# Modulation products cut by column group and turned by VectorE, with two early blocks of layer 1 in the slots of the gate weights

## What is computed

```python
def modulation(cvec, w_ada, b_ada):
    m = jax.nn.silu(cvec) @ w_ada + b_ada
    return jnp.split(m, 6, axis=-1)
...
        sh1p, sc1p, g1p, sh2p, sc2p, g2p = modulation(c_ctx, w_ada[i], b_ada[i])
        sh1s, sc1s, g1s, sh2s, sc2s, g2s = [m[:, None, :] for m in modulation(c, w_ada[i], b_ada[i])]
        hp = rmsnorm(xp, norm_g[i, 0]) * (1.0 + sc1p) + sh1p
        hs = rmsnorm(xs, norm_g[i, 0]) * (1.0 + sc1s) + sh1s
```

## Time and profile before

| | us |
|---|---|
| median of 3 runs | 1181.83 |
| lowest and highest of them | 1177.47, 1183.61 |
| span of the profiled execution | 1179.7 |
| start and first head, before scan 0 opens | about 54 |
| eight scans, 54 to 306 us of the span | about 252 |
| gates, output, norm and routing of layer 0 | 306 to 412 |
| experts of layer 0 | 412 to 640 |
| attention's projections | 640 to 790 |
| attention units | 790 to 860 |
| the rest of layer 1 | 860 to 1180 |

### The profile page before, as it was taken

How to read it: one execution, slowest core, us unless ns; L and a number is a source line. 1 busy time by engine, 2 the same in 40 slices (tenths; PEclk the granted TensorE clock), 3 DMA queues, 4 the chain that set the end, 5 groups by cost and what they waited for, 6 DMA issues and landing times.

```text
span 1179.7 us, 19786 instructions
## 1 busy us (share of the span) xinstructions
PE 1110.8 (94%) x8488; PEld 659.2 (56%) x8488; DVE 414.1 (35%) x1058; ACT 229.0 (19%) x530; POOL 128.1 (11%) x226
## 2 busy tenths in 40 slices
PE   4999999998999999999998899989989899999996
PEld 2666666665444666666563444434545756666552
DVE  2155555655712340000113654307843320000104
ACT  3111101101211411111111311126632311111110
POOL 0343433433100000000002000000000000000003
PEclk9999999999999999999999999999999899999999
DMA  9985444446941579999999942246751499999996
GB/s 345 307 277 157 115 144 144 144 144 216 379 160 67 179 277 422 426 426 426 427 424 339 389 167 76 89 161 215 282 218 44 155 378 429 426 425 424 426 418 228
DMA packets 101888, 321.26 MB, mean 272 GB/s; under 512 B 3985, under 2 KB 39105, under 8 KB 86433
## 3 DMA queue, kind: packets, MB, share of 16 engines
q1 hardware_dynamic: 93296, 298.05, 66.0%
q0 software_dynamic: 3248, 10.87, 2.7%
q10 hardware_dynamic: 5248, 10.98, 2.4%
HBM read 305.73 MB, written 14.16 MB: 271 GB/s over the span
## 4 chain that ended last, share of the span: by engine, by line
PE 74%; DMA 15%; DVE 4%; issue 2%; ACT 2%; SPq 2%; POOL 1%; POOLq 0%; ACTq 0%; DVEq 0%
PE bank L741 14%; PE bank L893 11%; PE bank L1088 11%; DMA ring<-in_moe_w_down 8%; PE bank L636 7%; PE bank L763 6%; PE bank L730 4%; PE bank L902 4%; PE bank L1019 4%; PE bank L531 3%; DMA ring<-in_moe_w_up 3%; DMA ring<-in_w_ada 2%; PE bank L918 2%; PE bank L622 1%; DMA ring<-expert_rows,moe_row 1%
## 5 line engine op out<-in xcount | busy, mean ns | idle before, releaser
L741 PE MATMUL bank<-ring,xn 128*64 128x256 f32 x1536 | 170.3, 380 | 4.6 <-DMA ring<-in_moe_w_up 4.2
L741 PEld LDWEIGHTS bank<-ring,xn 128*64 128x64 f32 x1536 | 110.0, 137 | 67.8 <-DMA ring<-in_moe_w_up 7.3
L893 PE MATMUL bank<-uT,ring 128*128 128x384 f32 x384 | 135.0, 496 | 0.0
L1088 PE MATMUL bank<-ring,uT 128*128 128x512 f32 x288 | 128.7, 601 | 4.6 <-DMA ring<-in_attn_w_qkv 3.0
L1802 DVE TENSOR_TENSOR moe_hh<-xn,bank 128x256 f32<-128x256 f32 x32 | 13.5, 421 | 299.0 <-ACT xn L1281 298.9
L1088 PEld LDWEIGHTS bank<-ring,uT 128*128 128x128 f32 x288 | 54.0, 192 | 69.0 <-issue 64.7
L893 PEld LDWEIGHTS bank<-uT,ring 128*128 128x128 f32 x384 | 69.3, 190 | 41.2 <-issue 1.1
L763 PE MATMUL bank<-ring,xn 128*64 128x512 f32 x384 | 85.5, 596 | 1.8 <-ACT xn L1287 1.6
L636 PE MATMUL bank<-ring,uT 128*128 128x512 f32 x192 | 84.0, 593 | 0.0
L730 PE MATMUL bank<-moe_g,moe_h 128*128 128x128 f32 x672 | 82.5, 281 | 0.8 <-DVE moe_g L1692 0.8
L730 PEld LDWEIGHTS bank<-moe_g,moe_h 128*128 128x128 f32 x672 | 78.7, 195 | 5.8 <-issue 5.8
(11 more groups left out here) (289 smaller groups left out, 1304.2 us busy)
## 6 DMA issues: line engine op xcount, KB each, us to landing
ring<-in_w_ada SPq DMA_DIRECT2D x24, 2048.0 KB, 10.0
ring<-in_moe_w_gate SPq DMA_DIRECT2D x24, 2048.0 KB, 18.5
ring<-in_moe_w_up SPq DMA_DIRECT2D x24, 2048.0 KB, 22.2
ring<-in_moe_w_down SPq DMA_DIRECT2D x20, 2048.0 KB, 25.2
ring<-in_hgrn_w_in SPq DMA_DIRECT2D x32, 512.0 KB, 7.8
moe_ring<-in_moe_w_gate SPq DMA_DIRECT2D x8, 2048.0 KB, 22.3
moe_ring<-in_moe_w_up SPq DMA_DIRECT2D x8, 2048.0 KB, 25.3
moe_ring<-in_moe_w_down SPq DMA_DIRECT2D x8, 2048.0 KB, 21.6
```

The source lines that it names most:

```text
L741: last = mm(bank[2 + e][64 * g:64 * g + 64, 256 * part:256 * part + 256], m["xe"][:, k, 64 * e:64 * e + 64], cols(slot)[:, k, 256 * g:256 ...
L893: last = mm(to[:, 0:TOK], w[:, k, f, :], uT[:, k, :], start=(k == 0), stop=(k == KC - 1))
L1088: last = mm(bank[b % 2][:, :], uT[:, k, t * P:(t + 1) * P], cols(slot)[:, k, :], start=(k == 0), stop=(k == KC - 1))
```

## The change

Three things are changed.

1. The product of a block is cut by output columns. Column group g gets, of each of the four 128-column parts of the block, the 32 columns that belong to it, and adds up all eight slices of the input. That is 32 matmuls of 128 columns, the moving operand read in four runs of 32. The bank then holds whole sums, in 128 columns.
2. VectorE turns the bank itself, by a transpose in blocks of 32x32, straight to SBUF, and adds the bias. ScalarE's copies and TensorE's transposes of the blocks are gone. Where TensorE had these transposes it now has, in scans 1 to 7, before the first gate matmul and in attention, a wait for the finished columns (`mod_cols`), since the bank is read by VectorE.
3. Early blocks 0 and 1 of layer 1 are loaded into slots 2 and 3 in the first scans. The gate weights follow into the same slots after these products, in the last scan. Early blocks 2 and 3 take slots 4 and 0, and each early product has its own bank.

```diff
-        EARLY_SLOTS = ((4, 4, 240), (0, 5, 96), (5, 4, 272), (4, 5, 256))
+        EARLY_SLOTS = ((2, 1, 32), (3, 1, 32), (4, 4, 240), (0, 5, 96))
+        EARLY_BANKS = (1, 2, 3, 0)
...
             head(1, 5, 0)
-            block512(0, 2, a["hgrn_w_in"][0], 8, 1)
-            block512(0, 3, a["hgrn_w_in"][0], 9, 1)
+            for b in range(2):
+                slot, before, _ = EARLY_SLOTS[b]
+                ada(1, slot, b, before)
...
-            for b in range(EARLY):
+            for b in range(2, EARLY):
                 slot, before, _ = EARLY_SLOTS[b]
                 ada(1, slot, b, before)
             for b in range(2):
-                block512(0, 4 + b, a["hgrn_w_out"][0], b, 6 - b)
+                block512(0, 2 + b, a["hgrn_w_in"][0], 8 + b, 2)
+            for b in range(2):
+                block512(0, 4 + b, a["hgrn_w_out"][0], b, 5 - b)
...
             def modulation_products(slot, to):
 
-                for r in range(2):
+                for k in range(KC):
+                    weights = cols(slot)[:, k, :].rearrange("p (j g l) -> p g j l", j=4, g=4)
                     for g in range(4):
-                        last = mm(bank[to][32 * g:32 * g + 32, :], cT[:, 2 * g + r, :], cols(slot)[:, 2 * g + r, :],
-                                  start=(r == 0), stop=(r == 1))
+                        last = mm(bank[to][32 * g:32 * g + 32, 0:P], cT[:, k, :], weights[:, g, :, :],
+                                  start=(k == 0), stop=(k == KC - 1))
                 return last
...
+                if at >= 2:
+                    need(pe, 0, "mod_cols", at - 1)
+                ada_block(FIRST_BLOCKS[at], 0, 6 + at % 2)
...
+                modulation_products(slot, EARLY_BANKS[blk]).then_inc(used[0][slot], 1)
...
+                if part in (0, 1, 3, 5):
+                    early_product((0, 1, None, 2, None, 3)[part])
...
                 if h >= 1:
-                    need(pe, 1, "mod_raw", h)
+                    need(pe, 1, "mod_cols", EARLY + h)
                 modulation_products(slot, 4).then_inc(used[1][slot], 1)
...
                 if before is not None:
-                    turn_mod(0, None, raw, 1 - b, 6, before + 5)
+                    need(pe, 0, "mod_cols", before + 5)
                 if following:
                     following(0)
...
             scan(7, 1, 3, early_part, 6)
-            turn_mod(0, 11, raw, 1, 6, 12)
+            need(pe, 0, "mod_cols", 12)
...
-            def block_columns(n, blk, to, count):
-
-                need(dve, n, "mod_T", count)
-                turned_columns(n, blk, to)
-
-            def turned_columns(n, blk, to):
-
+            def block_columns(n, blk, to, slot, uses, turned):
+
+                dve.wait_ge(used[n if blk >= EARLY else 0][slot], uses)
+                own(v.transpose(turned, bank[to][:, 0:P]))
                 bias = bias_col[:, 48 * n + 4 * blk:48 * n + 4 * blk + 4].unsqueeze(2).broadcast_to([P, 4, 2])
-                parts_of = bank[to][:, :].rearrange("p (j g r) -> p j r g", j=4, g=4)[:, :, 0:2, :]
-                own(v.tensor_reduce(adaln[:, n, blk, :, :], parts_of, X_AXIS, ALU.add))
-                v.tensor_tensor(adaln[:, n, blk, :, :], adaln[:, n, blk, :, :], bias, ALU.add).then_inc(S[n]["mod_cols"], 1)
+                v.tensor_tensor(adaln[:, n, blk, :, :], turned.rearrange("p (j r) -> p j r", j=4)[:, :, 0:2], bias, ALU.add)\
+                    .then_inc(S[n]["mod_cols"], 1)
```

More of the change, by code:

```diff
@@ L1014, in g_tile @@
                 if t == 0:
-                    pe.wait_ge(full[0][2 + half], 32)
+                    pe.wait_ge(full[0][2 + half], 48)
                 else:
@@ L1052, in _ @@
             count = experts(0)
-            raw = AT["raw"]
             def turn_features(t):
@@ L1200, in modulate @@
                     last.then_inc(S[n][name], 1)
-            def raw_out(n, raw, b, to, slot, uses, turned):
-                act.wait_ge(used[0][slot], uses)
-                if turned is not None:
-                    need(act, n, "mod_T", turned)
-                A(raw[:, b, :], bank[to][:, :], ACT.Copy).then_inc(S[n]["mod_raw"], 1)
             def gate_out(n, which, q, src):
@@ L1325, in _ @@
             for half in range(2):
-                for at_block in (2 * half, 2 * half + 1):
-                    raw_out(0, HG["raw"], at_block % 2, 6, FIRST_BLOCKS[at_block], 1, at_block - 1 if at_block >= 2 else None)
                 need(act, 0, "mod_ready", half + 1)
@@ L1372, in _ @@
                 head_out(i * 2 + 1, 1, i * 2)
-                rest_out(i * 2, 0, i)
+                rest_out(i * 2)
                 head_out(i * 2 + 2, 0, i * 2 + 1)
-                rest_out(i * 2 + 1, 1, i)
+                rest_out(i * 2 + 1)
             head_out(7, 1, 6)
-            rest_out(6, 0, 3)
-            for blk in range(EARLY):
-                early_raw(blk)
-            rest_out(7, 1, 3)
+            rest_out(6)
+            rest_out(7)
             act.wait_ge(hg["states"], 8)
@@ L1933, in scan @@
                 if before is not None:
-                    block_columns(0, before + 4, 6, before + 5)
+                    block_columns(0, before + 4, 5, 1 - b, before // 2 + 2, HG["raw"][:, 1 - b, 0:P])
                 take(bank[4], 2 * LEVELS).then_inc(hg["free_f"], 1)
@@ L1985, in _ @@
             for blk in range(EARLY):
-                dve.wait_ge(hg["next_T"], blk + 1)
-                turned_columns(1, blk, (1, 2, 3, 0)[blk])
-            block_columns(0, 11, 6, 12)
+                slot, before, _ = EARLY_SLOTS[blk]
+                block_columns(1, blk, EARLY_BANKS[blk], slot, before + 1, HG["raw"][:, blk % 2, 0:P])
+            block_columns(0, 11, 5, 1, 5, HG["raw"][:, 0, 0:P])
             dve.wait_ge(hg["o_out"], 8)
```

92 lines of the change are left out of this document (15 added, 77 removed).

## The result

| | before | after |
|---|---|---|
| median, us | 1181.7 | 1202.1 |
| lowest and highest | 1177.5, 1183.6 | 1196.0, 1205.3 |
| span of the profiled execution | 1179.7 | 1198.4 |

The change makes the kernel slower by 1.5%: the ratio is 1.0153, with a 95% interval from 1.0121 to 1.0184. I had forecast 1188, with a range up to 1197. The direction was right and the size was too small by two thirds.

A forecast was written before the change was run, and what follows sets the result against it. TensorE bounds scans 0 to 6; loops through several engines bound the last scan and attention. 8.1 + 0.6 + 0 - 0.4 - 2.2 + 0.1 = +6.2 us, with 2.1 around the span, gave 1188 us, range 1181 to 1197.

The forecast's parts named there:

- The six stalls: Opening of scans 1 to 6: TensorE's projection waits for VectorE's columns, 1.35 us later each, +8.1 us in all.
- The product: Modulation product cut into 64 instructions: 1.93 us, +0.08 each (0 to +0.2), +0.6 over scans 0 to 6.
- The rival of the weight loads: Modulation products: 48 more weight loads each come into the open, +0.42 us a product, 1194.5 us; chance 0.10.
- the last scan at 0: Last scan: two new waits, +1.2 and +0.9 us, offset by a lost DMA wait, low clock and slack; 0, from -2 to +3.
- The DMA wait of 0.61: Last scan: the third early product's 0.61 us wait for its weights goes under the new order of transfers.
- The start: Before scan 0: transposes after the last first block go, -0.43 us, product +0.08; -0.4 in all.
- Attention: Attention rounds: -0.2 us in each of eight, -0.6 for the last product; -2.2 in all, from 0 to -6.
- The rest of the span: After the last scores: -0.6 us for attention's last product, 0.10 more for VectorE's last block.
- Attention pays: Attention: ScalarE's wait bounds a round, which shrinks by up to 1.30 us, giving 1180 us; chance 0.12.
- The wait is hidden: Scans: VectorE comes early enough or TensorE catches up, so the 8.1 us falls away, 1180 us; chance 0.06.
- The clock falls behind the stalls: Scans: first projection part runs at half clock after each stall, 1.7 us, seven stalls +12, 1200 us; chance 0.12.

The follow-up runs named there:

- e1: Changed kernel with TensorE's wait for the block's columns moved behind the first projection part in every scan; 1192.0 us, ratio 1.0067.
- e5: Kernel before with only the four early products issued as 32 matmuls of 128 columns instead of 8 of 512; 1188.4 us, ratio 1.0038.
- e7: e1 with early products 2 and 3 rereading loaded blocks and gate and output weights asked for late; last scan's opening to last outputs 26.1 us.
- e10: Kernel before with only the four first products issued as 32 matmuls of 128 columns; one execution, scan 0 opens at 57.96 us.
- e8: e1 with attention's products written to banks 4 and 5 in turn; one execution, a round takes 7.44 us.
- e3: Kernel before with only the new load order: early blocks 0 and 1 in slots 2 and 3, gate weights later; 1184.1 us, ratio 1.0008.
- e4: Kernel before with only the product cut by output columns, ScalarE and TensorE still turning it, one transpose instead of four; 1184.4 us, ratio 1.0003.
- e2: Changed kernel with its third part undone, gate weights loaded in the first scans again; 1201.0 us, ratio 1.0159.
- e11: e8 with the wait for all twelve columns moved behind the first gate tile; one execution, gate tile starts 31.97 us after the last scan's opening.
- e6: e4 with the four first and four early blocks back to 8 matmuls of 512 columns and four transposes; 1179.0 us, ratio 0.9957.
- e9: e6 with attention's blocks turned by VectorE and their products written to two banks in turn; 1180.8 us, ratio 0.9976.

## Why the forecast was too low, point by point

In the spans of the traces the forecast of +6.2 us is 12.5 us short of the first execution and 9.8 short of the second. In both, 4.5 of these are the last scan.

- **The six stalls: right.** Forecast +8.1 with 1.35 us each, and +0.6 for the products; measured +8.4 in all (33.21 less 31.81 in each of six scans). The transpose takes 0.31 us where I took 0.28. The earlier trace rows gave the whole chain before the change was built. e1 shows it to be the cause.
- **The product: right.** 1.96 busy us for 64 instructions where 16 took 1.92. The rival of the weight loads falls. By the rule of the Trainium skill that the prediction sets beside it (page "TensorE: Matmul & The Clock Gate", section "Part 3: Packing small matmuls") it would have come true, and the trace goes against it.
- **The step that failed: the last scan at 0.** It measured +4.5 in both executions. Its two waits were in the sum, and their sizes were about right: the first early product starts 1.17 us later after the opening (2.08 for 0.91), where I had 1.2, and the gate tile 0.80 later after the last outputs (1.35 for 0.55), where I had 0.9. Against them I set some -2.1 for the stretch between: the DMA wait of 0.61, a low clock and slack. The DMA wait went, as foreseen, but the stretch measured +2.5 (28.9 us for 26.4). The gap of 1.85, 2.91 in the second execution, was in no term, and the low clock did not go. The product is cut into four times the instructions, I costed that by the columns streamed and the pace of issue, and asked nowhere whether the instructions themselves arrive in time. The earlier trace rows shows that TensorE can issue 24 of them at 9 ns each, and I read it as though it could do so forever. Opposite the 851 instructions of 28 us the changed kernel has 1254 in 32, in the stretch where its DMA engines are fullest. e5 measures this term alone, +4.0 us, and e7 shows most of it to be the queue.
- **The start: -0.4 forecast, +2.4 and +0.8 measured.** The same thing was left out here: the transposes that go are gone, but the loads that decide there land 1.2 us later with the cut, behind a packet of instructions (e10). The rest is the clock, which varies by execution.
- **Attention: -1.6 forecast for this row, -1.7 and -1.0 measured.** That the first comes so near is luck. The low clock at its start lasts 3.4 us in the first execution and 6.8 in the second and in the kernel before, so -1.0 is the like comparison. I had a round at 7.9, and it is 8.04. The mechanism was right, and its size was off: I put the new wait at 0.42 us a round, and it idles 0.58 and costs 0.60 (e8), against a gain of 0.66 (8.10 less 7.44) that I had put at 0.8. The 0.42 was counted with every other step in its old place. My reading, not tested apart, is that as those steps moved up, TensorE came to the wait sooner and met VectorE where it had been.
- **Gates to first scores, +3.0: mostly the clock, and not the change.** The kernel before took 485.3 us there, the changed one 488.4 and 488.3. But e3, e5 and e10, which have the code of before in this stretch, took 488.0, 488.4 and 487.5. Of the 3.0 us, 2.5 lie between the first gate tile and the first expert product, and there the traces sort by the granted clock. Where it is 0.50 for 3.4 us (the kernel before and e4) this part takes 114.4 us. Where it is so for 6.8 us (e2, e3, e5, e10, e11 and the second execution of the changed kernel) it takes 115.7 to 116.6, and for 10 to 11 us (the first execution, e1, e6, e8, e9) 116.9 to 117.7. e7, whose loads come late here, is left out. So the execution of the kernel before that I measured against was a short one here. The last 0.6 us stay open.
- **The rest of the span: -0.5 forecast, +2.1 and +0.4 measured.** A difference that does not repeat, and that I can't lay to the change.
- **The rivals.** "Attention pays" is wrong by its own measure, a round of 8.04. "The wait is hidden" is wrong by the 10.1 us of L852. "The clock falls behind the stalls" is wrong where it was put (1.00 in the scans), but the low clock in the last scan stayed, and grew from 3.4 to 10.3 and 6.8 us, around gaps that I had not foreseen.

## What to carry to other kernels

Place a wait directly ahead of the instruction that needs it, not ahead of independent work that could cover it: the same wait cost 10 us in front of the projection and nothing behind it. When an operation is split, count its instructions as well as its columns, above all where TensorE runs short instructions while weights fill the DMA queues. Apply such a cut only in dense stretches, and give a product whose reader is late a second bank.

## What the runs showed of the hardware

- TensorE's instructions are loaded in blocks of 16 KB by the same DMA engines as the data. Where they fall behind, the engine stands still in the middle of a run of plain matmuls, for 0.3 to 4.9 us, and the profile calls it "issue". The `q8 instruction` packets show it: in all 22 gaps of the last scans TensorE goes on 1.2 to 1.5 us after a packet has ended.
- The reverse holds too: one such packet, 1.1 us on one of 16 DMA engines, goes with a load of 2 MB that lands 1.1 to 1.4 us later, the last of its 16 parts alone.
- The same cut pays in one place and costs 4 us in another: with the three transposes that it saves, a scan is 0.3 us shorter (e4), the last scan 4 to 5 us longer (e5, e4).
- In the last scan, where TensorE's work is sparse, the granted clock falls to 0.50 for some us, ahead of the gap in one execution, and in or behind it in others. Between the gates and the experts it is at 0.50 for 3.4 to 11 us by execution, and this part takes 114.4 to 117.7 us with it. Six stalls of 1.7 us between dense projections left it at 1.00.
- VectorE turns 128x128 fp32 out of PSUM, in blocks of 32x32, in 0.31 us.
- 64 weight loads of 32 columns in one product of 64 matmuls stay hidden: 1.95 us against 1.92 for 16.
